# Feed-forward up projections with the high and low halves of the activations side by side in one matmul, and one weight split of the first block's last round moved

## The reference

```
def swiglu_ffn(h, w_gate_up, w_down):            # first block, D_FF = 2816
    gu = h @ w_gate_up
    return (jax.nn.silu(gu[..., :D_FF]) * gu[..., D_FF:]) @ w_down
...
for layer in range(DEPTH_2):                     # second block, two layers, D_FF_2 = 4096
    ...
    hf = rms_norm_2(x, ffn_norm[layer])
    x = x + jnp.square(jax.nn.relu(hf @ ffn_w1[layer])) @ ffn_w2[layer]
```

## Time and profile before

| what | value |
|---|---|
| median of three runs | 860.78 us (859.71 to 861.10) |
| the profiled execution, its own time | 861.04 us |
| its span, first to last instruction | 859.2 us |
| granted TensorE clock, mean | 0.996 of full speed (2.4 GHz) |
| PE busy | 846.7 us, 99% of the span |
| DVE busy | 539.2 us, 63% |
| ACT busy | 432.9 us, 50% |
| DMA | 148.71 MB, mean 173 GB/s |

### The profile page before, as it was taken

One profiled execution on the slowest core, in us unless ns is written; L12 is line 12 of the kernel. 1 busy time (PEld: TensorE's weight loads), 2 busy tenths in 40 slices (PEclk: granted clock), 3 DMA queues, 4 the chain that ended last, 5 costly groups with the idle time before them and its releaser, 6 DMA issues.

```text
span 859.2 us, 13974 instructions
## 1 busy us (share of the span) xinstructions
PE 846.7 (99%) x5674; PEld 763.7 (89%) x5674; DVE 539.2 (63%) x582; ACT 432.9 (50%) x584; POOL 47.3 (6%) x117
## 2 busy tenths in 40 slices
PE   8999999999999999999999999999999999999996
PEld 8877999999998799889999999999868999999995
DVE  5897654444448687986855555567587475555553
ACT  6675533443335686555644444446664454444431
POOL 3100000000000211200000000013000000000000
PEclk9999999999999999999999999999999999999999
DMA  9744355545554574345775555444524385555501
GB/s 335 279 147 149 123 196 195 195 160 188 189 196 151 193 249 147 106 160 168 233 241 175 186 192 191 121 141 148 169 83 149 97 268 182 188 190 180 184 32 50
DMA packets 92183, 148.71 MB, mean 173 GB/s; under 512 B 4497, under 2 KB 71585, under 8 KB 91761
## 3 DMA queue, kind: packets, MB, share of 16 engines
q1 hardware_dynamic: 90608, 143.90, 50.0%
q0 software_dynamic: 1248, 4.02, 1.5%
q10 hardware_dynamic: 288, 0.27, 0.1%
HBM read 147.10 MB, written 1.05 MB: 172 GB/s over the span
## 4 chain that ended last, share of the span: by engine, by line
PE 92%; DVE 3%; ACT 2%; DMA 2%; issue 1%; SPq 1%; DVEq 0%; POOLq 0%; POOL 0%; ACTq 0%
PE bank L1918 29%; PE bank L1919 28%; PE bank L1920 28%; DMA w_raw<-laid_swa_w_in_blocks 2%; ACT arena L1138 1%; PE bank L1990 1%; PE bank L2313 1%; PE bank L2096 1%; PE bank L2115 1%; DVE arena L1852 1%; PE bank L2598 0%; PE bank L2285 0%; PE bank L2132 0%; DVE arena L1361 0%; DVE arena L1866 0%
## 5 line engine op out<-in xcount | busy, mean ns | idle before, releaser
L1192 DVE TENSOR_TENSOR w_lo<-w_raw,w_hi 128x2048 fp32r<-128x2048 f32 (+2 forms) x126 | 282.7, 2251 | 150.6 <-ACT w_hi L681 150.4
L1918 PE MATMUL bank<-xT_hi,w_hi 128*128 128x256 f32 x1068 | 304.9, 286 | 0.3
L1919 PE MATMUL bank<-xT_lo,w_hi 128*128 128x256 f32 x1068 | 302.8, 283 | 0.0
L1920 PE MATMUL bank<-xT_hi,w_lo 128*128 128x256 f32 x1068 | 302.8, 283 | 0.0
L681 ACT ACTIVATE w_hi<-w_raw 128x2048 fp32r<-128x2048 f32 (+1 forms) x128 | 239.5, 1878 | 93.4 <-PE bank L1920 85.6
L1918 PEld LDWEIGHTS bank<-xT_hi,w_hi 128*128 128x128 f32 x1068 | 204.5, 192 | 5.7 <-issue 3.1
L1919 PEld LDWEIGHTS bank<-xT_lo,w_hi 128*128 128x128 f32 x1068 | 204.7, 192 | 2.0 <-issue 0.2
L1920 PEld LDWEIGHTS bank<-xT_hi,w_lo 128*128 128x128 f32 x1068 | 204.6, 192 | 0.2
L1918 PE MATMUL bank<-w_hi,ff_hi 128*128 128x512 f32 x344 | 134.6, 391 | 0.0
L1919 PE MATMUL bank<-w_lo,ff_hi 128*128 128x512 f32 x344 | 134.3, 390 | 0.0
L1920 PE MATMUL bank<-w_hi,ff_lo 128*128 128x512 f32 x344 | 133.9, 389 | 0.0
(11 more groups left out here) (264 smaller groups left out, 724.9 us busy)
## 6 DMA issues: line engine op xcount, KB each, us to landing
w_raw<-in_ffn_w SPq DMA_DIRECT2D x64, 1024.0 KB, 5.3
w_raw<-in_ffn_w_gate_up SPq DMA_DIRECT2D x22, 1024.0 KB, 5.1
w_raw<-in_ab_w_in SPq DMA_DIRECT2D x12, 1024.0 KB, 7.2
w_raw<-in_ffn_w_down SPq DMA_DIRECT2D x11, 1024.0 KB, 5.2
w_raw<-in_swa_w_out SPq DMA_DIRECT2D x4, 1024.0 KB, 7.6
w_raw<-in_ab_w_out SPq DMA_DIRECT2D x4, 1024.0 KB, 4.9
w_raw<-in_c_w_out SPq DMA_DIRECT2D x4, 1024.0 KB, 5.1
w_raw<-laid_swa_w_in_blocks SPq DMA_DIRECT2D x3, 1024.0 KB, 13.5
```

The source lines that it names most:

```text
L1192: dve.tensor_tensor(view(w_lo, ch), view(w_raw, ch), view(w_hi, ch).bitcast(F32), ALU.subtract).then_inc(S["lo_done"], 1)
L1918: pe.matmul(out, sh, mh, start=first, stop=False)
L1919: pe.matmul(out, sh, ml, start=False, stop=False)
L1920: return pe.matmul(out, sl, mh, start=False, stop=last)
```

## The change

The two halves of the transposed activations, which were two tensors, become one, `xT`, in which for each block k of inputs the 256 high columns and the 256 low columns are neighbours. `xT_hi` and `xT_lo` are now views of it. A new function, `feature_stacked`, issues two matmuls in each of the 16 places instead of three: one of `w_hi` against all 512 columns of `xT[:, k]`, and one of `w_lo` against the 256 high ones, accumulated on the first half of the bank. A feature block now fills a bank, with the main sum in its first half and the cross term in its second, so a chunk takes two banks (gate 0 and 1, up 2 and 3).

The two halves are added by a DVE `tensor_reduce` over pairs that lie 256 columns apart, which reads 1024 values of two banks and writes 512 to a new buffer `ff_g`. ACT's `silu` and `relu` and DVE's product then read `ff_g`.

The steady loops use it: 8 turns of the loop of `ffn1` with a gate and an up chunk each, and in each `squared_relu` the chunks c[3] and c[5] and 5 turns of two chunks. The last turn of that loop is now written out, with the old `feature_major`. The first two chunks of each phase and the last ones stay as they were. Before c[3] of `squared_relu` PE newly waits for the second `relu`.

```diff
-        xT_hi = sb("xT_hi", [P, NT, KT, P], F32R)
-        xT_lo = sb("xT_lo", [P, NT, KT, P], F32R)
+        xT = sb("xT", [P, KT, 2, NT, P], F32R)
+        xT_hi = xT[:, :, 0].rearrange("p k t c -> p t k c")
+        xT_lo = xT[:, :, 1].rearrange("p k t c -> p t k c")
...
+            def feature_stacked(ch, b):
+
+                hi, lo = view(w_hi, ch), view(w_lo, ch)
+                for f in range(2):
+                    for k in range(KT):
+                        pe.matmul(bank[b + f], hi[:, k, f * P:(f + 1) * P], xT[:, k].rearrange("p s t c -> p (s t c)"),
+                                  start=k == 0, stop=False)
+                        last = pe.matmul(bank[b + f][:, 0:SEQ], lo[:, k, f * P:(f + 1) * P],
+                                         xT[:, k, 0].rearrange("p t c -> p (t c)"), start=False, stop=k == KT - 1)
+                last.then_inc(S["mm_done"], 1)
...
             with pe.Fori(0, N1 - 3) as it:
-                gate(c[5], 2, it)
+                arrived(c[5], it, 3)
+                pe.wait_ge(S["ff1_sg"], 2 + it)
+                feature_stacked(c[5], 0)
                 down(c[6], 1, it)
                 arrived(c[7], it, 3)
-                feature_major(c[7], bank[1])
+                feature_stacked(c[7], 2)
...
+            def gate_sum(ch, i, it=0):
+                dve.wait_ge(S["mm_done"], ch.index + 1 + 3 * it)
+                dve.tensor_reduce(ff_g[:], main_and_cross(0), axis=AX, op=ALU.add).then_inc(S["ff1_gs"], 1)
+
+            def hidden_of_sum(ch, i, it=0, then=None):
+                dve.wait_ge(S["ff1_sg"], i + 1 + it)
+                dve.wait_ge(S["mm_done"], ch.index + 1 + 3 * it)
+                dve.tensor_reduce(ff_g[:], main_and_cross(2), axis=AX, op=ALU.add).then_inc(S["ff1_us"], 1)
+                dve.wait_ge(S["ff1_us"], i - 1 + it)
+                dve.tensor_tensor(ff_h[:], ff_act[:], ff_g[:], ALU.mult).then_inc(S["ff1_h"], 1)
+                if then:
+                    low(then)
+                dve.wait_ge(S["ff1_hi"], i + 1 + it)
+                dve.tensor_tensor(ff_lo[0][:], ff_h[:], ff_hi[0][:].bitcast(F32), ALU.subtract).then_inc(S["ff1_lo"], 1)
...
+                pe.wait_ge(S["ff2_relu"], N2 * f + 2)
+                up2_stacked(c[3], 0)
                 down2(f, c[4], 1, 1)
-                up2(c[5], 1)
-                with pe.Fori(0, N2 // 2 - 2) as it:
+                up2_stacked(c[5], 1)
+                with pe.Fori(0, N2 // 2 - 3) as it:
                     down2(f, c[6], 2, 0, it)
-                    up2(c[7], 0, it)
+                    up2_stacked(c[7], 0, it)
                     down2(f, c[8], 3, 1, it)
-                    up2(c[9], 1, it)
+                    up2_stacked(c[9], 1, it)
...
                 with dve.Fori(0, N2 // 2 - 2) as it:
+                    up_sum(f, c[3], 2, it)
                     low(c[6], it, 4)
                     hidden2(f, 2, 0, it)
                     low(c[7], it, 4)
+                    up_sum(f, c[5], 3, it)
                     low(c[8], it, 4)
                     hidden2(f, 3, 1, it)
                     low(c[9], it, 4)
```

More of the change, by code:

```diff
@@ L206, in build @@
         squares = take(P, NT, DM)
+        ff_g = take(P, 2, SEQ)
         used[0] = 0
@@ L719, in transposed_high @@
                     act.wait_ge(S["t_psum"], 4 * (n - 1) + 2 * t + half + 1)
-                    act.activation(xT_hi[:, t, 4 * half:4 * half + 4, :].rearrange("p k c -> p (k c)"),
-                                   bank[2 * t + half][:], ACT.Copy).then_inc(S["xTh_ready"], 1)
+                    act.activation(xT_hi[:, t, 4 * half:4 * half + 4, :],
+                                   by_k(bank[2 * t + half]), ACT.Copy).then_inc(S["xTh_ready"], 1)
             def enter(use, n, then):
@@ L832, in silu_gate, with silu_of_sum @@
                                ACT.Silu).then_inc(S["ff1_sg"], 1)
+            def silu_of_sum(i, it=0):
+                act.wait_ge(S["ff1_gs"], i - 1 + it)
+                act.activation(ff_act[:], ff_g[:], ACT.Silu).then_inc(S["ff1_sg"], 1)
             def hidden_high(i, it=0, buf=0):
@@ L858, in _ @@
                 high(c[10], it, 3)
-            silu_gate(c[-7], N1 - 2)
+            silu_of_sum(N1 - 2)
             high(c[-4])
+            high(c[-3])
             hidden_high(N1 - 2)
-            for ch in c[-3:]:
+            for ch in c[-2:]:
                 high(ch)
@@ L1011, in relu_square, with relu_square_of_sum @@
                 act.activation(ff_hi[buf][:], ff_act[:], ACT.Square).then_inc(S["ff2_hi"], 1)
+            def relu_square_of_sum(f, i, buf, it=0):
+                act.wait_ge(S["ff2_sum"], (N2 - 4) * f + i - 1 + 2 * it)
+                act.wait_ge(S["ff2_lo"], N2 * f + i + 2 * it)
+                act.activation(ff_act[:], ff_g[:], ACT.Relu).then_inc(S["ff2_relu"], 1)
+                act.wait_ge(S["ff2_relu"], N2 * f + i + 1 + 2 * it)
+                act.activation(ff_hi[buf][:], ff_act[:], ACT.Square).then_inc(S["ff2_hi"], 1)
             def squared_relu(f, after):
@@ L1218, in transposed_low @@
                     k = slice(4 * half, 4 * half + 4)
-                    dve.tensor_tensor(xT_lo[:, t, k, :].rearrange("p k c -> p (k c)"), bank[2 * t + half][:],
-                                      xT_hi[:, t, k, :].rearrange("p k c -> p (k c)").bitcast(F32),
+                    dve.tensor_tensor(xT_lo[:, t, k, :], by_k(bank[2 * t + half]), xT_hi[:, t, k, :].bitcast(F32),
                                       ALU.subtract).then_inc(S["xTl_ready"], 1)
@@ L1451, in hidden @@
                 dve.wait_ge(S["mm_done"], ch.index + 1 + 3 * it)
[L1452 removed]
+                dve.tensor_tensor(ff_h[:], ff_act[:], bank[2][:].rearrange("p (a b) -> p a b", a=2),
                                   ALU.mult).then_inc(S["ff1_h"], 1)
@@ L1480, in _ @@
             step(dve.tensor_tensor(both_gains, gain[:, 0], gain[:, 1], ALU.mult))
-            hidden(c[-5], N1 - 2)
-            for ch in c[-3:]:
+            hidden_of_sum(c[-5], N1 - 2, then=c[-3])
+            for ch in c[-2:]:
                 low(ch)
@@ L2219, in _ @@
             pe.wait_ge(S["ff1_h"], N1 - 1)
-            feature_major(c[-3], bank[1])
+            feature_major(c[-3], bank[2])
             down(c[-2], N1 - 2, ts=(0,))
```

30 lines of the change are left out of this document (23 added, 7 removed).

## The result

| | before | changed | ratio, 95% interval |
|---|---|---|---|
| first measurement | 860.94 us (859.71 to 861.12, 4 runs) | 855.24 us (854.68 to 856.12, 4 runs) | 0.994, 0.9928 to 0.9952 |
| the same kernel once more (`changed_again`) | 860.47 us (859.04 to 861.02, 9 runs) | 855.27 us (853.47 to 855.65, 5 runs) | 0.9943, 0.993 to 0.9957 |

By the medians the change makes the kernel faster by 5.7 and 5.2 us, and by the ratios, which are worked out together with their intervals, by 5.2 and 4.9 us. The forecast was 8.4. The time, 855.2, lies 0.2 us above the range. The profiled execution took 855.74 us against 861.04.

What follows compares the result with a forecast made beforehand. PE, busy for 99% at full clock, was taken as the bound. 861.04 - 8.0 (stacked chunks) - 0.35 (last round of `ffn1`) = 852.7 us for the profiled execution, 852.4 on the median; range 851 to 855.

Steps and rivals of the forecast that it cites:

- What bounds the kernel: Whole kernel: PE, busy for 99% at full clock, with 92% of the last-ending chain, so only PE's time counts.
- The pair: Stacked chunks on PE: two matmuls replace three, 347.5 instead of 360.0 ns, in 640 places, 8.0 us won.
- DVE: 40 new sums of 1.21 us, 48 us more DVE work, none on the path while the slacks hold.
- The slack before D: Loop of `ffn1`: time between `ff_lo` done and the down chunk's start, 3.49 us before, 2.04 us left.
- The last round: End of `ffn1`: two small PE stalls, for c[-3]'s `low` and for `ff_lo`, vanish with the new order, 0.35 us.
- the first stall: Last round of `ffn1`: PE waits for c[-3]'s `low`; would grow by 1.25 us in the old order.
- The fixed part stays: Rival on PE's matmuls: the 12.5 ns belong to a change of weights, so nothing is won there; 860.4 us, chance 4%.
- A wait eats part of it: Rival: a slack is smaller than worked out, say by a late weight split or load; half the gain, 856.4 us, chance 5%.
- The sum is slow: Rival: DVE's sums are costly and PE waits in `ffn1` and `ffn2`; at 6 us a sum about 894 us, chance 4%.

Runs made afterwards that it cites:

- both_512: Changed kernel, but w_lo too is multiplied with all 512 columns, adding the product of the two low parts; 919.36 us.
- cross_half: Changed kernel, but the 256-column matmul accumulates on the second half of the bank instead of the first; 855.14 us, one run.
- by_two: Changed kernel with stacked matmuls in the order 512, 512, 256, 256 columns; 850.32 us, ratio to before 0.9895.
- early_low: Changed kernel, but in the loop of `ffn1` the next up chunk's weights are split ahead of the rounding and `ff_lo`; 855.05 us, one run.
- sum_thrice: Changed kernel, but the up sum of `ffn1` is made three times, twice into an unused buffer, so that `ff_lo` comes later; 858.53 us.
- old_tail: Changed kernel, but the last round of `ffn1` in the old order, the split of c[-3] behind rounding and `ff_lo`; 856.00 us, one run.
- short_128: Changed kernel, but w_lo is multiplied with the first 128 columns only in the stacked chunks; 846.68 us.

## Why the prediction was wrong, point by point

**What bounds the kernel** was right. PE stayed at 99%, its chain at 92%, and all that was won or lost was won or lost on PE.

**The pair: this step failed**, as "A place had 3 x 120.0 = 360.0 ns and now has 227.5 + 120.0 = 347.5, so 12.5 ns less", with the reason that 12.5 "comes from exactly the widths that are exchanged". The widths were the right ones but their order was not: both paces came from streams of one width. In alternation a pair takes 352.5 ns where the three matmuls took 359.5 (chunks of 5.640 and 5.752 us), so it wins 7.0 ns and not 12.5, and 640 x 7.0 = 4.5 us and not 8.0. `both_512` (one width, no surcharge), `cross_half` (no effect) and `by_two` (347.8) show that it is the alternation and neither the layout, nor the bank, nor DVE's sums. The remaining unstacked chunks of the changed kernel keep their 5.75 to 5.76 us, so the layout of `xT` costs nothing, as was said. The bounds of the term, 0 to 9.1, held it. The range did not: it followed the chances, and all of the forecast's 87% stood at 12.5 or more, though no row of before showed two widths alternating. The lower bound ("the pair takes what the three took") was spent on a rival of 4%, and no slower or faster pair stood between.

**The longer D of `ffn1`** was in no term: 0.036 us for each of eight D, 0.3 us in all. It is absent in `by_two` and `both_512`, not DVE's doing (`early_low`), and absent in `ffn2` of the changed kernel, though a stacked chunk stands ahead of D there too. So alternation ahead of D is needed but doesn't suffice; the cause stays open.

**DVE.** The sum takes 1.22 us (1.21 taken), and 40 of them 48.9 us. The page's total rises by 42.3 only: where DVE now works without a pause, as in `ffn2`, the records of neighbouring instructions overlap by some 0.08 us, and the total counts the overlap once. The slack before D is 2.11 us (2.04), of which `sum_thrice` shows some 1.95 to be usable. No wait for a sum, a `low` or the second `relu` stands in the loops.

**The last round** was right: -0.36 for -0.35. The remark that the old order beside stacked chunks would grow the first stall, 0.18 us, by 1.25 was right as well (`old_tail`: 1.44 there, and 0.20 at the second place).

**The rivals.** "The fixed part stays" is refuted: `by_two` takes 347.8 ns a place, though it changes weights as often as the kernel before, twice. The 12.5 ns are no fixed price of an instruction either: the first pair behind D has 226.7 and 113.3 ns, both 0.443 ns a column with nothing on top. "A wait eats part of it" named the size (856.4) nearly right and the mechanism wrong; there is no wait. That the range, which was stretched into this case, was missed by only 0.2 us is therefore luck. "The sum is slow" did not happen. The Trainium skill, "TensorE: Matmul & The Clock Gate", section "Back-to-back issue gap", calls N / 2.4 + 2.5 ns its gap for isolated matmuls and says that in a real stream the weight load takes part in setting the spacing. By that gap, which the prediction set against the rows, the 640 instructions are worth an estimated 1.6 us. Neither order bears that out: even the alternating pair wins nearly three times as much. The pace and the weight loads of `short_128` fit the sentence on the weight load.

**The sum with the measured terms**: 4.5 - 0.3 + 0.36 = 4.6 us from the traces, against 5.2 (4.1 to 6.2) and 4.9 (3.7 to 6.0) by the ratios. Had the kernel taken two in a row, the three feed-forwards would have won 507.44 - 498.99 = 8.45 us, where the prediction's terms make 8.35. That they meet so closely is partly luck: the stacked chunks win 7.5 us and not 8.0, and the 0.5 us that is missing comes from 31 D that are 0.017 shorter, which no term had.

## What to carry to other kernels

A pace read from a stream of equal matmuls holds for such a stream; where a change interleaves two shapes, price the pair as unknown, between the sum of the two paces and what it replaces, and widen the range by that. When two widths must share a bank, try the orders: two long and two short in a row cost a few lines of code and gave 3.9 us more in the feed-forwards than one and one. And before work is added to an engine beside the critical one, work out its slack in the chain (here 2.0 of 3.5 us were to be left) and not from its busy share; it held to 0.1 us.

## What the runs showed of the hardware that was not expected

**Order of widths.** At the same instructions, columns and banks, a chunk of 16 long and 16 short matmuls takes 5.640, 5.563, 5.587 or 5.559 us with one, two, four or eight in a row (in `ffn2`). The D behind it takes 5.467, 5.450, 5.487 or 5.467, which puts two in a row ahead of eight.

**A floor for short matmuls.** Beside a matmul of 512 columns, one of 128 adds some 110 ns to the pair and not the 66 of the line, and the weight loads there are 108 to 109 ns apart. The starts themselves are 280 ns apart after the 512 and 60 after the 128, so only their sum is a price.

**The clock between `ffn1` and `ffn2a`.** That stretch, which the change doesn't touch, takes 125.7 to 125.9 us or 127.2 us, in kernels of either kind. Ahead of the difference stand four matmuls of 4 rows that keep PE for 1.9 us. The windows of the changed kernel, and then of the same kernel in `changed_again`, over the chunk behind them (columns as above; the granted clock is the third figure from the end):

```profile
332.60:339.90 7.30, 7.30 (x49) 7.30 (x49) 4.19 (x3) 7.24 (x13) 2.50 (x10) 0.77 0.45 146
```

```profile
331.80:337.60 5.80, 5.80 (x49) 5.80 (x49) 4.20 (x3) 5.75 (x12) 1.17 (x5) 1.00 0.44 154
```

The timeline of PE in the changed kernel there:

```profile
330.67 1.98 PE L2343 MATMUL bank<-x_norm,sel 4*128 4x512 f32 x4
...
333.18 0.42 PE L1963 MATMUL bank<-xT,w_hi 128*128 128x256 f32 x1
333.40 0.41 PE L1964 MATMUL bank<-xT,w_hi 128*128 128x256 f32 x1
```

In the one execution the starts are 0.21 us apart, the 1.2 GHz level, for nearly half of the chunk's time (a mean granted clock of 0.77), and in the other the clock stays at 2.4 GHz: 1.45 us between two executions of one program. PE was never idle there; what it did before was work with 4 of 128 rows. It did the same in the executions without the dip, so that work alone doesn't explain it. The profiled executions of the kernel before and of the changed kernel (the first ones) both have the dip, so it isn't in their difference, but it makes single times of one kernel differ by that much, which is why effects under 1.5 us were read from the traces here.
